# A diffusion layer on one core: x is loaded ahead of the modulation weights, which come in four column pieces

## The reference, cut to what matters

```python
sh1, sc1, g1, sh2, sc2, g2 = ada_mod(c, w_ada[l], b_ada[l])          # silu(c) @ w_ada + b_ada, cut in six
sh1c, sc1c, ... = ada_mod(c_ctx[None], w_ada[l], b_ada[l])           # the same for the context
u = x * (1.0 + sc1) + sh1                                            # modulate(x, sh1, sc1), per channel
proj = u @ w_in                                                      # 1024 channels to 2576 columns
x_lru = centred_dwconv(x_lru, conv_w, conv_b)                        # width 4, on the first 512 columns
```

## Time and profile before

| | |
|---|---|
| median of 3 runs | 2358.86 us (2356.47 to 2365.62) |
| profiled execution | 2360.09 us, its span 2358.4 us |
| PE busy | 2179.8 us, 92% of the span |
| DVE, ACT, POOL busy | 1019.9, 467.2, 446.0 us |
| moved by DMA | 510.55 MB, mean 216 GB/s |
| mean granted clock of PE | 0.962 |

### The profile page before, as it was taken

How to read it: one execution, slowest core, us unless ns; L and a number is a source line. 1 busy time by engine, 2 the same in 40 slices (tenths; PEclk the granted TensorE clock), 3 DMA queues, 4 the chain that set the end, 5 groups by cost and what they waited for, 6 DMA issues and landing times.

```text
span 2358.4 us, 33076 instructions
## 1 busy us (share of the span) xinstructions
PE 2179.8 (92%) x9927; PEld 1013.3 (43%) x9928; DVE 1019.9 (43%) x1580; ACT 467.2 (20%) x624; POOL 446.0 (19%) x417
## 2 busy tenths in 40 slices
PE   6889999879968999999998899999998999999992
PEld 3444444464544444443443344444443444444441
DVE  3575754465775243444334243433253333323234
ACT  2334434331220111111111111111111111111113
POOL 0010100001231122222222232312123222122110
PEclk8989999889968999999999999999999999999996
DMA  8222221012252676889489999647899458886634
GB/s 331 82 64 71 89 72 36 1 73 86 87 214 97 242 293 217 298 288 399 136 287 399 353 358 402 238 158 246 315 385 354 170 197 283 304 307 234 235 87 171
DMA packets 168969, 510.55 MB, mean 216 GB/s; under 512 B 16434, under 2 KB 51002, under 8 KB 167770
## 3 DMA queue, kind: packets, MB, share of 16 engines
q1 hardware_dynamic: 153802, 474.25, 53.8%
q0 software_dynamic: 15120, 35.67, 6.8%
HBM read 480.51 MB, written 31.46 MB: 217 GB/s over the span
## 4 chain that ended last, share of the span: by engine, by line
PE 85%; DVE 7%; DMA 4%; issue 2%; ACT 1%; SPq 1%; DVEq 0%; POOLq 0%; POOL 0%
PE psall L591 27%; PE psall L619 14%; PE psall L595 10%; PE psall L762 10%; PE psall L623 5%; PE psall L600 4%; PE psall L750 3%; PE psall L873 2%; PE psall L867 2%; DMA arena<-in_w_down_dram 2%; PE psall L660 1%; PE psall L729 1%; PE psall L628 1%; DMA arena<-in_x_dram 1%; DVE arena L1389 1%
## 5 line engine op out<-in xcount | busy, mean ns | idle before, releaser
L591 PE MATMUL psall<-arena 128*128 128x512 f32 x1472 | 646.2, 597 | 24.4 <-issue 23.6
L591 PEld LDWEIGHTS psall<-arena 128*128 128x128 f32 x1472 | 278.9, 191 | 370.2 <-issue 370.2
L619 PE MATMUL psall<-arena 128*128 128x512 f32 x736 | 323.9, 598 | 6.5 <-DVE arena L1756 3.5
L595 PE MATMUL psall<-arena 128*64 128x512 f32 x1152 | 257.2, 598 | 9.2 <-DMA arena<-in_w_up_dram 4.4
L1584 DVE STREAM_TRANSPOSE arena<-arena 128x1024 f32<-128x1024 f32 x49 | 61.0, 1246 | 454.5 <-PE psall L591 276.5
L762 PE MATMUL psall<-arena 128*128 128x512 f32 (+1 forms) x608 | 246.6, 563 | 0.7 <-ACT arena L1006 0.7
L619 PEld LDWEIGHTS psall<-arena 128*128 128x128 f32 x736 | 139.7, 191 | 185.3 <-issue 185.3
L1186 ACT COPY arena<-psall 128x512 f32<-128x512 f32 x49 | 28.7, 586 | 790.1 <-PE psall L660 790.1
L1756 DVE COPY arena<-psall 128x512 f32<-128x512 f32 x49 | 33.9, 691 | 322.5 <-PE psall L660 322.4
L762 PEld LDWEIGHTS psall<-arena 128*128 128x128 f32 x608 | 116.5, 192 | 120.7 <-issue 116.4
L1189 ACT ACTIVATE arena<-arena 128x1024 f32<-128x1024 f32 x49 | 51.8, 1057 | 583.8 <-DVE arena L1592 583.8
(11 more groups left out here) (306 smaller groups left out, 2079.0 us busy)
## 6 DMA issues: line engine op xcount, KB each, us to landing
arena<-in_w_gate_dram SPq DMA_DIRECT2D x128, 1024.0 KB, 6.6
arena<-in_w_up_dram SPq DMA_DIRECT2D x128, 1024.0 KB, 8.2
arena<-in_w_down_dram SPq DMA_DIRECT2D x128, 1024.0 KB, 8.6
arena<-in_w_ada_dram SPq DMA_DIRECT2D x16, 1024.0 KB, 5.2
arena<-in_w_ada_dram SPq DMA_DIRECT2D x4, 2048.0 KB, 14.5
arena<-in_w_in_dram SPq DMA_DIRECT2D x16, 512.0 KB, 4.1
arena<-in_x_dram SPq DMA_DIRECT2D x2, 2048.0 KB, 27.9
arena<-in_w_out_dram SPq DMA_DIRECT2D x1, 4096.0 KB, 13.9
```

What stands on the lines that cost most here:

```text
L591: mm = pe.matmul(ps[2 * g + s], xT[:, k, :], w[:, s * BANK:(s + 1) * BANK], start=(k == 0), stop=(k == KD - 1))
L595: mm = pe.matmul(ps[2 * g][HT * j:HT * j + HT, :], xT[:, k, 0:HT], w[:, j * BANK:(j + 1) * BANK], start=(k == 0), stop=(k == KD - 1), skip ...
L619: mm = pe.matmul(ps[6 + s], aT[:, k, :], w[:, s * BANK:(s + 1) * BANK], start=(k == 0), stop=(k == KD - 1))
```

## The change

The loads of x and ctx and the first `w_in` tile go ahead of the modulation weights. These now come in four pieces of 512 columns (256 of the shift and the same 256 of the scale, two transfers of 1 MB each with rows of 1 KB), each over all 1024 channels, so piece q yields shift and scale for the channel blocks 2q and 2q+1. The x transposes go first on PE, in a ring of three banks, and are copied out as they are. ACT and DVE then apply scale and shift to `uT` in place, ACT to block 2q, DVE to block 2q+1. Jobs 0 to 2 run together, two channel blocks at a time, behind each piece. The rows of a piece lie in four column groups as partial sums, so turning them (L691) is now a product with a small matrix `pair_of` that adds the four; for that `arow1` is cleared first. The bias broadcast waits for the fourth turn instead of the only one.

```diff
@@ -127,12 +127,13 @@
         AL = reg(O_AL, L)
-        wada1 = [reg(off, 2, 4 * BANK) for off in (0, 4096, O_U, O_U + 4096)]
+        wada1 = [reg(off, KD, BANK) for off in (0, 4096, O_XL, O_L + P)]
         AS = 2 * P
...
         prow = reg(O_L, P)
+        pair_of = small[:, 60:62]
         xin = reg(O_QT, NT + NTC, D)
...
@@ -359,8 +360,11 @@
+        def uT_bank(n):
+            return ps[(4, 6, 7)[n % 3]]
+
         def uT_in(n):
-            v = ps[4 + n % 4]
+            v = ps[(4, 6, 7)[n % 3]]
             return v[:, :].rearrange("p (r w) -> p r w", w=GRID_W) if n < 16 else v[:, 0:CTX]
...
@@ -435,8 +439,6 @@
             wada_v = w_ada[0].rearrange("(k p) n -> p k n", p=P)
-            for j in range(4):
-                sp.dma_start(wada1[j], wada_v[:, 2 * j:2 * j + 2, 0:4 * BANK]).then_inc(d_wada[j], 16)
             x_v = x[0].rearrange("(t p) d -> p t d", p=P)
...
@@ -455,7 +457,12 @@
-            for n in range(WRING):
+            proj_tile(0)
+            for c_ in range(4):
+                for h in range(2):
+                    sp.dma_start(wada1[c_][:, :, 2 * P * h:2 * P * h + 2 * P],
+                                 wada_v[:, :, D * h + 2 * P * c_:D * h + 2 * P * c_ + 2 * P]).then_inc(d_wada[c_], 16)
+            for n in range(1, WRING):
                 proj_tile(n)
...
@@ -465,11 +472,11 @@
             ada_piece(0)
-            sp.wait_ge(arow1_out, 1)
+            sp.wait_ge(arow1_out, 4)
             sp.dma_start(ada_flat, b_ada[0:1, 2 * D:6 * D].partition_broadcast(P).rearrange("p a n -> p (a n)")).then_inc(d_bada, 16)
...
                 sp.dma_start(wa_sb[32 * j:32 * j + RANK, :, :], gla_wa[0].rearrange("d r n -> r d n")).then_inc(d_lruw, 16)
-            sp.wait_ge(ada_used, 1)
+            sp.wait_ge(ada_used, 4)
             sp.dma_start(wv, win_v[:, :, CV:CV + BANK]).then_inc(d_wv, 16)
...
@@ -668,37 +675,56 @@
             pe.wait_ge(cs_ready, 1)
-            for k in range(KD):
-                if k % 2 == 0:
-                    pe.wait_ge(d_wada[k // 2], 16)
-                for j in range(4):
-                    mm = pe.matmul(ps[1][32 * j:32 * j + 2, :], csil[:, k, :], wada1[k // 2][:, k % 2, j * BANK:(j + 1) * BANK],
-                                   start=(k == 0), stop=(k == KD - 1), skip_group_check=True)
-            mm.then_inc(ada_used, 1)
-
-            def turn_ada():
-                pe.wait_ge(arow1_ready, 4)
-                for q in range(2 * KD):
-                    j, m = q // 4, q % 4
-                    r = slice(32 * j, 32 * j + 2)
-                    mm = pe.transpose(ps[j][:, 2 * m:2 * m + 2], arow1[r, m * P:(m + 1) * P], ident[r, r])
+            def ada_columns(q):
+                pe.wait_ge(d_wada[q], 32)
+                if q:
+                    pe.wait_ge(ada1_ready, q)
+                for k in range(KD):
+                    j = k % 4
+                    mm = pe.matmul(ps[5][32 * j:32 * j + 2, :], csil[:, k, :], wada1[q][:, k, :],
+                                   start=(k < 4), stop=(k >= 4), skip_group_check=True)
+                mm.then_inc(ada_used, 1)
+
+            def turn_ada(q):
+                pe.wait_ge(arow1_ready, 4 * q + 5)
+                for m in range(4):
+                    mm = pe.matmul(ps[5][:, 2 * m:2 * m + 2], arow1[:, m * P:(m + 1) * P], pair_of, start=True, stop=True,
+                                   skip_group_check=True)
                 mm.then_inc(arow1_out, 1)
-            n = 0
-            for grp, (t0, t1) in enumerate(((0, 4), (4, 8), (8, 10))):
+            def turn_x(n):
+                grp, k = n // KD, n % KD
+                t0, t1 = ((0, 4), (4, 8), (8, 10))[grp]
                 pe.wait_ge(d_x[grp], 16)
-                for k in range(KD):
-                    if n == 4:
-                        turn_ada()
-                    if n >= 4:
-                        pe.wait_ge((uT_act, uT_dve)[n % 2], (n - 4) // 2 + 1)
-                    for i, t in enumerate(range(t0, t1)):
-                        mm = pe.transpose(ps[4 + n % 4][:, i * P:(i + 1) * P], xin[:, t, k * P:(k + 1) * P], ident[:, :])
-                    mm.then_inc(x_turned, 1)
-                    n += 1
-
-            pe.wait_ge(uT_act, 12)
-            pe.wait_ge(uT_dve, 12)
+                if n >= 3:
+                    pe.wait_ge((uT_act, uT_dve)[(n - 3) % 2], (n - 3) // 2 + 1)
+                for i, t in enumerate(range(t0, t1)):
+                    mm = pe.transpose(uT_bank(n)[:, i * P:(i + 1) * P], xin[:, t, k * P:(k + 1) * P], ident[:, :])
+                mm.then_inc(x_turned, 1)
+
+            def first_jobs(k0, k1):
+                for k in range(k0, k1):
+                    pe.wait_ge((uT_act, uT_dve)[k % 2], 13 + k // 2)
+                    for i in range(3):
+                        _, _, seg, n = jobs[i]
+                        mm = pe.matmul(ps[i][0:P, 0:seg[1] - seg[0]], wring[0][:, k, 0:P], uT[:, k, seg[0]:seg[1]],
+                                       start=(k == 0), stop=(k == KD - 1))
+                        if k == KD - 1:
+                            mm.then_inc(proj_done, 1)
+
+            for n in range(16):
+                turn_x(n)
+            ada_columns(0)
+            for n in range(16, 24):
+                turn_x(n)
+            turn_ada(0)
+            pe.wait_ge(d_win[0], 16)
+            for q in range(4):
+                if q < 3:
+                    ada_columns(q + 1)
+                first_jobs(2 * q, 2 * q + 2)
+                if q < 3:
+                    turn_ada(q + 1)
...
@@ -738,7 +764,7 @@
                     decay_logits(0, i)
-                if what != "job":
+                if what != "job" or i < 3:
                     continue
...
@@ -995,16 +1021,30 @@
             act.activation(small[:, 0:8], small[:, 0:8], ACT.Exp, scale=-1.0).then_inc(cs_ready, 1)
-            act.wait_ge(ada_used, 1)
-            for j in (0, 2):
-                act.copy(arow1[32 * j:32 * j + 2, :], ps[1][32 * j:32 * j + 2, :]).then_inc(arow1_ready, 1)
-            act.wait_ge(ada1_ready, 1)
+            def rows_out(q):
+                act.wait_ge(arow1_ready, 1)
+                act.wait_ge(ada_used, q + 1)
+                for j in (0, 2):
+                    act.copy(arow1[32 * j:32 * j + 2, :], ps[5][32 * j:32 * j + 2, :]).then_inc(arow1_ready, 1)
+
+            def modulated(k):
+                act.wait_ge(ada1_ready, k // 2 + 1)
+                act.activation(uT[:, k, 0:SEQ], uT[:, k, 0:SEQ], ACT.Identity,
+                               bias=ada1[:, 0, k, 0:1], scale=ada1[:, 1, k, 0:1])
+                act.activation(uT[:, k, SEQ:L], uT[:, k, SEQ:L], ACT.Identity,
+                               bias=ada1[:, 0, k, 1:2], scale=ada1[:, 1, k, 1:2]).then_inc(uT_act, 1)
+
             for n in range(0, 24, 2):
-                grp, k = n // 8, n % 8
-                w, c0, who = (512, 512 * grp, 0) if grp < 2 else (256, 1024, 1)
+                if n == 16:
+                    rows_out(0)
                 act.wait_ge(x_turned, n + 1)
-                act.activation(uT_out(n), uT_in(n), ACT.Identity,
-                               bias=ada1[:, 0, k, who:who + 1], scale=ada1[:, 1, k, who:who + 1]).then_inc(uT_act, 1)
+                act.copy(uT_out(n), uT_in(n)).then_inc(uT_act, 1)
+            act.wait_ge(uT_act, 12)
+            act.wait_ge(uT_dve, 12)
+            for q in range(4):
+                modulated(2 * q)
+                if q < 3:
+                    rows_out(q + 1)
...
@@ -1159,7 +1199,7 @@
                 if T == 0:
-                    act.wait_ge(ada1_ready, 2)
+                    act.wait_ge(ada1_ready, 5)
                 for b in range(2 if T + 1 < NT else 1):
...
@@ -1247,22 +1287,43 @@
             dve.tensor_scalar(ncl[:, :], small[:, 0:8], 8.0, None, ALU.mult).then_inc(cl_ready, 1)
-            dve.wait_ge(ada_used, 1)
-            for j in (1, 3):
-                dve.tensor_copy(arow1[32 * j:32 * j + 2, :], ps[1][32 * j:32 * j + 2, :]).then_inc(arow1_ready, 1)
-            dve.wait_ge(arow1_out, 1)
-            pada = psall[:, 0:4 * BANK].rearrange("p (j n) -> p j n", j=4)[:, :, 0:KD].rearrange("p j (k a) -> p j k a", a=2)
-            for a in range(2):
-                link(dve.tensor_tensor(ada1[:, :, :, a].rearrange("p s (h k) -> p (s h) k", h=2), pada[:, :, :, a],
-                                       par[:, C_BADA:C_BADA + 2 * KD].rearrange("p (j k) -> p j k", j=4), ALU.add))
-            dve.tensor_scalar(ada1[:, 1], ada1[:, 1], 1.0, None, ALU.add).then_inc(ada1_ready, 1)
-            dve.wait_ge(ada1_ready, 1)
+            dve.wait_ge(const_ready, 1)
+            dve.memset(arow1, 0.0).then_inc(arow1_ready, 1)
+            link(dve.tensor_reduce(pair_of, ident[:, :].rearrange("p (j a) -> p a j", j=4)[:, 0:2, :], AX_X, ALU.add))
+
+            def rows_out(q):
+                dve.wait_ge(arow1_ready, 1)
+                dve.wait_ge(ada_used, q + 1)
+                for j in (1, 3):
```

(31 more changed lines are left out.)

## The result

The changed kernel takes 2368.2 us (median of 12 runs, 2364.3 to 2371.06) against 2360.09 us of the kernel before (12 runs in the same rounds). The ratio is 1.0031 with a 95% interval of 1.0022 to 1.0040, so it is slower, by 7 to 8 us, and within the half per cent that I called no change. I had forecast 2361.

A forecast was written before the change was run, and what follows sets the result against it. TensorE, busy 92% of the span, was taken to bound the kernel, so the first gate's shift is the total's. Gate at 75.9 against 73.64, 2.3 us later, gave 2362.4, or 2361 against the median; range 2351 to 2371.

The forecast's parts named there:

- a serial loop: Products, jobs' matmuls, turn and addition of each piece run in series; three rounds take 23.9 us.
- a later convolution: Before the first gate, VectorE starts 1.3 us after the jobs end; gate 10.0 us behind them instead of 6.67, loss 3.3.
- 10 us of small things: Upper end of the range: 10 of the 15 us of possible small delays added, giving 2371.
- A round at full clock: In the loop, one piece's products, six job matmuls, turn and addition in series: 7.98 us.
- a turn: Behind each piece's products, eight records of 2 columns with a full weight load on TensorE: taken as 1.0 us.
- the first modulation piece lands at 27.0: Loads at the start: first weight piece lands at 27.0 us, its short rows flowing at 381 GB/s, 5.5 us a piece.
- 1.90 us at full clock: TensorE's products of a modulation piece, 16 records: 1.90 us, so the first piece's end at 28.9.
- I charge one such fall, 2.4 us: TensorE's clock falls once at thin places of the loop, costing 2.4 us; jobs end at 65.9.
- modulated in the open, 1.4 us: After the third round the last two blocks are modulated with nothing covering it, 1.4 us, before the last job group.
- The rival that took the whole loop to stay low: TensorE stays below full clock in the loop: rounds of 14.8 us, gate some 27 us later, 2386 us; chance 6%.
- Behind the transfers: Rival: the four rounds hide in a piece's 5.5 us transfer; gate at 64.4, 9.2 us earlier, 2350 us; chance 5%.
- Several small things late: Rival: late broadcast, slower turn, two more clock falls, half-clock first products; together 15 us, chance 3% of passing half a per cent.

The follow-up runs named there:

- e3: Changed kernel with modulation rows alternating between two PSUM banks and the turn between the halves of a group's job matmuls; ratio 1.0003 to the kernel before.
- e2: Changed kernel with only jobs 0 and 1 in the loop and job 2 whole behind it; ratio 1.0022 to the kernel before.
- e7: Kernel before with x loaded first and modulated in place, but four old long-row weight pieces, one turn and jobs one after the other; ratio 1.0029.
- e4: Changed kernel with each modulation piece loaded in rows of 8 KB, so values differ; read only at the first gate, 3.4 us earlier than 80.67.
- e1: Changed kernel with jobs 0 to 2 taken out of the loop, run one after the other behind all modulation; ratio 1.0070 to the kernel before.
- e6: Changed kernel with two banks, turn between job halves, and job 2 split around the last group of jobs 0 and 1; ratio 1.0012 to the kernel before.
- e9: Changed kernel with two banks, late split job 2, four useless matmuls before first products, and bias broadcast issued right behind the pieces; ratio 0.9996 to the kernel before.
- d2: Kernel before the change with two useless clears on VectorE ahead of its first convolution; ratio 1.0022 to the kernel before.
- e5: Changed kernel with four useless matmuls ahead of the first products and two ahead of the last job group; ratio 1.0023 to the kernel before.
- d5: Kernel before the change with five useless clears on VectorE ahead of its first convolution; ratio 1.0011 to the kernel before.

## Why the prediction was right, and where it was short

**The direction and the reason held.** The forecast was a transfer wait and the transposes taken off TensorE's path and more than paid back by a serial loop and a later convolution. The size did not: I had said 2.3 us at the gate and it was 7.0. The time stays within the range, near its upper end, because I had let in 10 us of small things there; that is margin and not a good sum. e3 shows the loop: with its waits covered, and the falls of the clock gone, the gate comes 7.2 us earlier, at the place of before. e2 shows the convolution: the gate comes 6.9 behind the jobs instead of 9.8. e7 shows that x first alone gives nothing.

**The terms that measured as said.** A round at full clock 7.92 us (7.98 said; the first, with a low clock, 9.57); a turn 0.95 (1.0, between bounds of 0.3 and 1.8); bias and one 0.6; the x tiles copied out by 25.6 (26.4 said), under the wait for the piece, with waits of 0.3 us for a bank (three of them for four, a quarter fewer and not a third); from the jobs to the gate 9.8 (10.0); the broadcast 7.8 us from issue to landing (7.7), issued at 62.2 (59.5), so that it landed at about 70, 2 us ahead of the convolution's start. The gate's shift is nearly the whole's (7.0 of 7 to 8 us).

**The terms that were mis-sized.** The gate came at 80.67 and not at 75.9. Of the 4.8 us:
- "the first modulation piece lands at 27.0": it was waited for until 28.77. 1.7 us. I had 381 GB/s for short rows from half a microsecond of one transfer; over a whole piece they flow at 348, which is 6.0 us for 5.5, so 0.5 of it. The first half of x was waited for until 12.86 and not 12.3, another 0.5. The rest is not taken apart; executions differ by 0.8 here. e4, with long rows, came at 27.06.
- "1.90 us at full clock" for the first products: 3.59, after 4.18 us of idle. The granted clock was 0.50. 1.7 us. It is not there in each execution: e1, e2, e4, e6 had 1.90 at this place.
- "I charge one such fall, 2.4 us": there were two in the loop, at the second products (3.54 for 1.90) and in the last group (6.26 for 4.56), 3.3 us together. 0.9 us.
- "modulated in the open, 1.4 us": 1.24 and 0.58, 1.8 until the last group starts. 0.4 us. The row of another ScalarE line (1057 ns for 1024 elements) was not the price of this one.

The clock thus cost 5.0 us, where I had 2.4. The Trainium skill, TensorE: Matmul & The Clock Gate, "HAM oscillation — how this bites in real kernels", describes bursts of matmuls that are shorter than the transfer wait between them, and of which each starts cold. The trace agrees at the first piece (4.18 us of wait for the transfer, then 3.59 for 1.90), but not each time: the same products ran at full clock behind such a wait of 3.70 us in e1. The other two places (3.54 and 6.26) stand behind waits of 0.85 and 2.42 us for VectorE and ScalarE, which is not the case that the Trainium skill describes. The rival that took the whole loop to stay low was wrong: from 44 to 64 us the granted clock was 1.00.

**The rivals.** "Behind the transfers" fell: TensorE waits for VectorE in the loop, and e4 moved the first piece and left the rounds at 7.9 us. "Several small things late" is what in part came: one more fall of the clock and the first products at half clock, no late broadcast, no dear turn.

**What stays open.** The timed runs and the one profiled execution don't agree everywhere: e9 began the experts 2.8 us late in its profile and was timed level, d2 0.2 late and timed 5 us slower. The times of the single runs explain this in part: a profile is one execution of a spread. e9's took 2363.7 us where nine of its eleven runs took 2356.8 to 2358.9, and d2's was its fastest of seven. Of the seven profiles with 642 to 643 us behind the gate, five (e1, e5, e6, e7, e9) were the slowest of all their kernel's runs. The kernel before has such a spread too: of the thirty runs beside e9, 24 took 2356.6 to 2361.0 and six 2363.3 to 2365.6. So the table's two groups need not be traits of the kernels. What makes the clock fall behind one wait and not behind its like stays open, and with it whether a change can make it rarer; d2 and d5 don't settle it.

## What to carry to other kernels

When one late input is cut into pieces, add up what a round of the cut loop has in series and hold it against the time in which a piece lands: here products, turn, addition and matmuls made 7.9 us of it where a piece took 6.0 (2.1 MB at 348 GB/s), and a second bank and another order (e3) gave back the whole of what the change cost. That a round under 6.0 would have won is argued and not shown; no version had one with the jobs in it, and the best only drew level. Look too at who consumes the last result: three jobs that end together, where they ended one after the other, moved the next engine's start back by 3 us. And a thin stretch ahead of full matmuls should be priced with the clock that it may leave behind: three such places cost 5 us in this execution, where the whole net loss was 7.

## What the runs showed of the hardware that I had not expected

The clock can cost four microseconds far behind a change that touches nothing there: from the gate to the experts the same instructions took 638 us in seven executions and 642 to 643 in seven. One idle time of 2.34 us, behind the same work, was followed by full clock in seven executions and by half clock in seven, in two pairs of them at the same moment to 0.02 us. It sets a floor to what one profile of such a kernel can tell: before a few microseconds in one are explained, look where its time stands among the runs of its kernel.

With matmuls of no use ahead, the clock was full where it was needed (three places in e5, 4.5 us at the gate). The first two of these places were at full clock without them in e1, and the timing found no gain.

Rows of 1 KB flowed at 348 GB/s for the length of a piece, though a single transfer reached 381 for half a microsecond; a rate read from so short a window was too high to plan with here.
